# Twelve stages on one core: how each stage's semaphores are set back to zero

## The chip, the cores and the metric

The kernel runs on one core of one Trainium2 chip. The metric is the device time of one execution in microseconds (us); lower is better. Five engines work side by side, each with its own stream of instructions: TensorE (PE, with its weight loads PEld), VectorE (DVE), ScalarE (ACT), GpSimd (POOL) and SyncE (SP). SP computes nothing here: it issues most of the DMAs and handles semaphores. The engines know of each other only by semaphores, counters that one of them raises and another waits for.

## The reference, cut to what matters

All is computed in float32 on a sequence of 512 positions with 1024 features. Two layers of a first block (feed-forward, token mixing, feed-forward), then one layer of a second block (another token mixing, then a layer that picks 128 experts of 16384 for every position):

```python
def first_block(x, c, w_ada, b_ada, ...):
    c_act = jax.nn.silu(c)
    for l in range(DEPTH):                       # DEPTH = 2
        mod = (c_act @ w_ada[l] + b_ada[l])[:, None, :]
        sh0, sc0, g0, sh1, sc1, g1, sh2, sc2, g2 = jnp.split(mod, N_MOD, axis=-1)
        h = _rmsnorm(x, norm_g[l, 0]) * (1.0 + sc0) + sh0
        x = x + 0.5 * g0 * _swiglu(h, ffn_w_gate[l, 0], ffn_w_up[l, 0], ffn_w_down[l, 0])
        h = _rmsnorm(x, norm_g[l, 1]) * (1.0 + sc1) + sh1
        x = x + g1 * _token_mix(h, w_in[l], w_out[l], ...)
        h = _rmsnorm(x, norm_g[l, 2]) * (1.0 + sc2) + sh2
        x = x + 0.5 * g2 * _swiglu(h, ffn_w_gate[l, 1], ffn_w_up[l, 1], ffn_w_down[l, 1])
    return _rmsnorm(x, final_g)

def second_block(x, ...):
    for l in range(DEPTH_2):                     # DEPTH_2 = 1
        m = token_mix(x, w_in[l], ...)
        x = layer_norm(DEEPNORM_ALPHA * x + m, ln1_g[l], ln1_b[l])
        f = peer_ffn(x, peer_wq[l], peer_keys[l], peer_u[l], peer_v[l])
        x = layer_norm(DEEPNORM_ALPHA * x + f, ln2_g[l], ln2_b[l])
    return x
```

The change touches nothing of what is computed.

## The kernel before, in words

The activations stay in the core's on-chip memory (SBUF) from start to end, as `xT` (128 partitions x 8 tiles of features x 512 positions). The weights stream in from memory in tiles of 128 x 1024 numbers (512 KB). The class `Stream` moves a tile through a ring: SP loads it (`load`, the DMA at L242) into one of two raw buffers, ACT rounds it (`whi`, L252), POOL subtracts to get the rest (`wlo`, L256), and PE multiplies three times with the halves (L263 to L265), 24 matmuls to a tile. Three tiles are ready and a fourth has landed when a stage begins; `ahead` tells that to the new stage's counters, each engine raising those that are its own (SP raises `w_in`, the counters of landed tiles).

The program is a row of stages: `first_modulation`; then a hardware loop of two turns, one for each layer, over `ffn` (0), `proj_mix`, `soft_attention`, `out_proj` and `ffn` (1); then `second_mix` and `peer`. The loop's body stands in the program once, so all counters have to be zero again when the second turn comes. Each stage is one `nc.Block`: every engine jumps to its own part, runs it, and at the end all engines wait for each other (in listings, a wait for `barrier_..._release`). Inside a stage each engine's part is written out in order, so its order is that of the code.

Every stage takes its semaphores from the pool of the chip (`semaphores`, L91) and gives them back at its end, so that the next one gets the same ones. Before that, `clear` (L101) opens a block of its own with one part only, SP's, which sets them to zero one by one with `sem_clear` (L108). That block too ends with all engines waiting for each other. So between two stages there are two meetings of all engines, with SP's clears between them: 23 after `first_modulation`, 30 after `ffn`, 37 after `proj_mix`, 23 after `soft_attention`, 14 after `out_proj`, 47 after `second_mix`; none after `peer`. With the loop's two turns that is 12 clearing blocks in an execution.

PE keeps multiplying constants at the end of most stages and at the start of the next (`keep_busy`, L295; in `peer` L1973): work without a result, put there to hold up its clock.

Of the kernel before, what the change touches and what calls it, by code (L numbers as in the profile page):

```python
# [89 lines left out]

def semaphores(nc, ctx, names):  # L91

    sems = {}
    for n in names.split():
        n, _, many = n.partition("*")
        own = [ctx.enter_context(nc.semaphore(f"{n}{k}" if many else n)) for k in range(int(many or 1))]
        sems[n] = own if many else own[0]
    return sems

def clear(nc, sems):  # L101

    with nc.Block() as block:
        @block.sync
        def _(sp):
            for own in sems.values():
                for s in own if isinstance(own, list) else [own]:
                    sp.sem_clear(s)  # L108

# [23 lines left out]
def first_modulation(nc, T):  # L133

    ROWS = 8
    with ExitStack() as ctx:
        M = semaphores(nc, ctx, "lc_c lc_silu lc_const lc_x lc_par m_row*8 m_dot m_ch n_sq n_sum n_root n_rstd "
                                "w_in*2 w_hi w_lo")
# [4 lines left out]
        with nc.Block() as block:  # L143
# [53 lines left out]
            def _(dve):  # L197
# [15 lines left out]
                modulate(nc, T, link, 0)  # L213
        clear(nc, M)

S_SEMS = "w_in*2 w_hi w_lo w_mm "
# [145 lines left out]

FFN_T, PROJ_T, OUT_T = 2 * KF + 3 * KD, NZ, KD
LAYER_T = 2 * FFN_T + PROJ_T + OUT_T

def ffn(nc, T, layer, which):
# [10 lines left out]
    KL = 16  # L379
    with ExitStack() as ctx:  # L380
        M = semaphores(nc, ctx, N_SEMS + S_SEMS + Q_SEMS + "f_silu f_prod f_ahi f_act f_res f_par f_ch f_lam f_exp f_pre "
                                                           "m_row*3 m_early*2 m_dot m_raw")
        sb = lambda n, s, t=F32: ctx.enter_context(nc.sbuf_tensor(n + str(which), s, t))
# [25 lines left out]
        with nc.Block() as block:  # L409
            @block.sync  # L410
            def _(sp):
                W.ahead(sp=sp)
                if EARLY:
                    for g in range(2):
                        sp.dma_start(erow[:, g], T.d["ada"][mod_layer, 8 + g]).then_inc(M["m_early"][g], 16)
                    with sp.Fori(1, EARLY) as i:
                        for j in range(4):
                            W.load(sp, i, j)
                        for g in range(2):

                            sp.wait_ge(M["m_dot"], i * 4 + 2 * g - 1)
                            sp.dma_start(erow[:, g], T.d["ada"][mod_layer, i * 2 + 8 + g]).then_inc(M["m_early"][g], 16)
                with sp.Fori(max(EARLY, 1), KF // 2) as i:
                    for j in range(4):
                        W.load(sp, i, j)
                if which:
                    sp.dma_start(T.par[:, :], T.d["par"][1 - layer]).then_inc(M["f_par"], 16)
                for n in range(UP, UP + 3):
                    W.load(sp, n // 4, n % 4)
                rows = 0  # L430
                for o in range(KD):
                    while rows < dots // 2 and 2 * rows < sum(split[:o + 1]):
                        if rows < 3:

                            sp.wait_ge(M["w_mm"], UP + 4)
                        else:
                            sp.wait_ge(M["m_dot"], 4 * EARLY + 2 * (rows - 3) + 3)
                        sp.dma_start(wrow[:, rows % 3], T.d["ada"][mod_layer, col0 // 2 + rows]
                                     ).then_inc(M["m_row"][rows % 3], 16)
                        rows += 1  # L440
                    for n in range(UP + 3 + 3 * o, min(UP + 6 + 3 * o, FFN_T + 4)):
                        W.load(sp, n // 4, n % 4)
                W.load(sp, (FFN_T + 3) // 4, 3)
                for n in (2, 3):
                    W.landed(sp, FFN_T + n)
# [67 lines left out]
            def _(dve):  # L513
# [67 lines left out]
                Q.rstd(dve)  # L581
        clear(nc, M)

# [5 lines left out]
def proj_mix(nc, T, layer):  # L589

    with ExitStack() as ctx:
        M = semaphores(nc, ctx, N_SEMS + S_SEMS + "n_h p_rope p_wt p_tmm p_tout z_act z_dve "
                                "r_w r_rot r_t1 r_rope r_ch r_var r_root r_tri r_vn r_gelu r_sq r_sg r_y r_sig "
# [37 lines left out]
        with nc.Block() as block:  # L631
            @block.sync
            def _(sp):
                W.ahead(sp=sp)
                sp.dma_start(wtok, T.d["wtok"][layer]).then_inc(M["p_wt"], 16)
# [173 lines left out]
            def _(dve):  # L809
# [93 lines left out]
                for a in range(2):  # L903
                    dve.wait_ge(M["z_act"], ROPED + a + 1)
                    dve.wait_ge(M["r_y"], a + 1)
                    nc.vector.tensor_tensor(T.y[:, a], T.z[:, GU + a], T.y[:, a], ALU.mult)
        clear(nc, M)

def soft_attention(nc, T):  # L910
# [16 lines left out]
    with ExitStack() as ctx:  # L927
        M = semaphores(nc, ctx, "a_s a_nm a_e a_pr a_ch a_t a_te a_pv a_o "
                                "a_cs a_cm a_ce a_cp a_ct a_cte a_gate b_sq b_sum b_mean b_root b_wide b_mm b_y")
# [23 lines left out]
        SUM0 = 256  # L953
        with nc.Block() as block:
            @block.tensor
            def _(pe):
# [156 lines left out]
            def _(dve):  # L1113
# [109 lines left out]
                out(TILES - 1)  # L1223
        clear(nc, M)

def out_proj(nc, T, at):

    with ExitStack() as ctx:
        M = semaphores(nc, ctx, S_SEMS + Q_SEMS + "x_hi x_lo o_res o_pre")  # L1230
        yh = ctx.enter_context(nc.sbuf_tensor("o_yh", [P, KD, S], F32R))
# [8 lines left out]
        with nc.Block() as block:  # L1240
            @block.sync
            def _(sp):
                W.ahead(sp=sp)
                for n in range(4, OUT_T + 4):
# [42 lines left out]
            def _(dve):  # L1287
# [6 lines left out]
                Q.rstd(dve)  # L1294
        clear(nc, M)

# [6 lines left out]
def second_mix(nc, T):  # L1303
# [19 lines left out]
    with ExitStack() as ctx:  # L1323
        M = semaphores(nc, ctx, S_SEMS + "x_f x_hi x_lo p_wt v_tmm z_act z_dve "
                                "v_w v_pad v_diag v_ch v_conv v_dmm v_dc v_win v_pool v_mu v_cen v_sq v_var v_root v_rcp "
# [51 lines left out]
        with nc.Block() as block:  # L1377
            @block.sync
            def _(sp):
                W.ahead(sp=sp)  # L1380
                sp.dma_start(pw[:, :, :], T.d["pw"]).then_inc(M["v_w"], 16)
# [269 lines left out]
            def _(dve):  # L1651
# [127 lines left out]
                nc.vector.reciprocal(T.rstd[:, :], T.rstd[:, :]).then_inc(M["l_r"], 1)  # L1779
        clear(nc, M)  # L1780

# [45 lines left out]
def peer(nc, T):  # L1827
# [12 lines left out]
    with ExitStack() as ctx:  # L1840
        M = semaphores(nc, ctx, S_SEMS + f"x_t x_n x_hi x_lo e_keys e_q e_sc e_sv e_top e_ch e_x e_xo g_uv*{LOW + TOPS + EARLY} "
                                "g_dot g_gelu g_w g_diag g_mm g_ln g_al g_ch g_st g_cp g_rt g_fin g_out h_dif h_exp h_pick")
# [29 lines left out]
        with nc.Block() as block:  # L1872
            @block.sync
            def _(sp):
                W.ahead(sp=sp)
                for n in range(4, NQ2):
# [301 lines left out]
def build(nc, d):  # L2178

    T = Tensors()  # L2180
    T.d = d
    with ExitStack() as ctx:
        sb = lambda n, s: ctx.enter_context(nc.sbuf_tensor(n, s, F32))
# [49 lines left out]
def first_block(nc, T):  # L2233

    with ExitStack() as c1:
# [5 lines left out]
        T.raw = s1("raw", [P, 112])  # L2241
        T.lam = s1("lam", [P, 16])
        first_modulation(nc, T)
        with nc.Fori(0, L) as layer:
            ffn(nc, T, layer, 0)
# [152 lines left out]
```

## Time and profile before

| | |
|---|---|
| median of 3 executions | 3887.87 us (3886.22 to 3887.95) |
| the profiled execution, its own time | 3886.95 us |
| its span, from first to last instruction | 3885.2 us |
| mean granted clock of TensorE | 0.962 of full speed |
| PE busy | 3486.6 us, 90% of the span |
| DVE, POOL, ACT busy | 56%, 41%, 31% |
| DMA | 839.57 MB, mean 216 GB/s; 421 GB/s in most of `peer` |

The stages of the profiled execution, from the timeline (us from the span's start): `first_modulation` to 45, `ffn` 47 to 416, `proj_mix` 419 to 581, `soft_attention` 584 to 720, `out_proj` 722 to 774, `ffn` 775 to 1145; the second turn 1151 to 2250; `second_mix` 2253 to 2465; `peer` 2468 to 3885. In a table of windows each row gives, for one stretch, the busy time of every engine with its number of instructions in brackets, then the granted clock of PE (1.00 is full speed), the share of the DMA engines and the GB/s moved. In a timeline each row gives a start, a length, the engine, the line of the code, the operation, and in square brackets how long the engine had been idle and what ended that. "PEq L103" there stands for the clearing block: the wait ended when all had come to its end.

### The profile page before, as it was taken

What the parts mean: (1) busy time and instruction counts of PE and PEld (TensorE: products, weight loads), DVE (VectorE), ACT (ScalarE), POOL (GpSimd) and SP (SyncE); (2) the same over time, 40 slices, a digit from 0 to 9 for tenths busy, and PEclk for the clock granted to TensorE, in tenths of its full rate; (3) what the DMA queues carried; (4) which work ended last, traced back from release to release, by engine and by line L of the source; (5) the groups of instructions that cost most, each with busy time, mean ns of one, the idle gap of its engine ahead of it and who ended that gap; (6) DMA issues with size and microseconds to landing.
All of it is one profiled execution on the core that took longest, in us unless ns stands there. A gap on an engine that the chain in (4) does not pass through costs nothing. (4 is left out here: it accounts for less than half of the span.)

```text
span 3885.2 us, 41685 instructions
## 1 busy us (share of the span) xinstructions
PE 3486.6 (90%) x13886; PEld 2361.7 (61%) x13886; DVE 2174.4 (56%) x4271; ACT 1216.5 (31%) x2225; POOL 1606.3 (41%) x960
## 2 busy tenths in 40 slices
PE   6999999899999999999999999897778778777777
PEld 4888676688878887766788876663333333333332
DVE  6546257433326455466333265478677777667664
ACT  3332226443323323145333233432222222222221
POOL 3446330244545455210444632335444444444442
PEclk9999999999999999999999999998998998999998
DMA  6526320122435454200223421269999999999996
GB/s 243 194 95 259 110 98 1 45 97 97 166 126 184 146 201 179 98 17 16 88 97 112 179 82 49 93 255 408 421 422 421 421 421 422 421 421 421 420 420 275
DMA packets 141434, 839.57 MB, mean 216 GB/s; under 512 B 15824, under 2 KB 16464, under 8 KB 63952
## 3 DMA queue, kind: packets, MB, share of 16 engines
q0 software_dynamic: 73728, 536.90, 33.5%
q1 hardware_dynamic: 67536, 300.56, 21.5%
q8 instruction: 87, 1.43, 0.2%
q14 instruction: 83, 0.68, 0.1%
HBM read 835.31 MB, written 2.10 MB: 216 GB/s over the span
## 5 line engine op out<-in xcount | busy, mean ns | idle before, releaser
L256 POOL TENSOR_TENSOR wlo<-wraw,whi 128x1024 fp32r<-128x1024 f32 x357 | 906.2, 2543 | 1462.9 <-ACT whi L252 1462.6
L252 ACT ACTIVATE whi<-wraw 128x1024 fp32r<-128x1024 f32 x357 | 377.4, 1058 | 663.4 <-DMA wraw<-in_wts 371.8
L263 PE MATMUL f_ps<-f_hh,whi 128*128 128x512 f32 x1408 | 550.3, 391 | 0.9 <-DVE f_hl L352 0.9
L264 PE MATMUL f_ps<-f_hl,whi 128*128 128x512 f32 x1408 | 548.2, 389 | 0.0
L265 PE MATMUL f_ps<-f_hh,wlo 128*128 128x512 f32 x1408 | 548.1, 389 | 0.0
L1967 PE MATMUL g_psF<-g_low,g_diagb 128*128 128x512 f32 x660 | 327.6, 650 | 101.0 <-ACT g_diagb L2025 100.9
L1967 PE MATMUL g_psF<-g_own,g_diagb 128*128 128x512 f32 x576 | 279.8, 636 | 71.9 <-ACT g_diagb L2025 71.9
L521 DVE TENSOR_TENSOR f_a<-f_sg,f_ps 128x512 f32<-128x512 f32 x88 | 60.5, 688 | 503.6 <-PE f_ps L265 487.1
L1967 PE MATMUL g_psF<-g_top,g_diagb 128*128 128x512 f32 x524 | 261.8, 651 | 72.3 <-ACT g_diagb L2025 72.2
L1967 PEld LDWEIGHTS g_psF<-g_low,g_diagb 128*128 128x128 f32 x660 | 134.7, 208 | 288.9 <-issue 288.9
L2019 ACT ACTIVATE g_dotb<-g_dotb 128x4 f32<-128x4 f32 (+1 forms) x134 | 27.5, 205 | 898.4 <-DVE g_dotb L2109 898.4
L263 PEld LDWEIGHTS f_ps<-f_hh,whi 128*128 128x128 f32 x1408 | 264.7, 188 | 60.0 <-issue 3.9
L264 PEld LDWEIGHTS f_ps<-f_hl,whi 128*128 128x128 f32 x1408 | 264.7, 188 | 55.1 <-issue 0.7
L265 PEld LDWEIGHTS f_ps<-f_hh,wlo 128*128 128x128 f32 x1408 | 264.6, 188 | 55.0
L1901 POOL DMA_INDIRECT g_low<-in_uv,idx x165 | 194.5, 1179 | 220.1 <-PE g_psF L1967 185.8
L2109 DVE CUSTOM_DVE_ANT_0 g_low<-g_low,xtok 128x1024 f32<-128x1024 f32 x165 | 199.6, 1225 | 106.9 <-DMA g_low<-in_uv,idx 104.1
L1967 PEld LDWEIGHTS g_psF<-g_own,g_diagb 128*128 128x128 f32 x576 | 115.5, 205 | 228.9 <-issue 228.7
L1901 POOL DMA_INDIRECT g_own<-in_uv,idx x144 | 169.5, 1177 | 189.1 <-PE g_psF L1967 161.2
L1967 PEld LDWEIGHTS g_psF<-g_top,g_diagb 128*128 128x128 f32 x524 | 107.1, 209 | 222.2 <-issue 222.2
L2109 DVE CUSTOM_DVE_ANT_0 g_own<-g_own,xtok 128x1024 f32<-128x1024 f32 x144 | 175.9, 1237 | 94.2 <-DMA g_own<-in_uv,idx 91.0
L1901 POOL DMA_INDIRECT g_top<-in_uv,idx x131 | 148.6, 1134 | 179.6 <-PE g_psF L1967 156.8
L130 DVE CUSTOM_DVE_ANT_0 m_prod<-m_wrow,crow 128x1024 f32<-128x1024 f32 x104 | 183.7, 1767 | 50.6 <-DMA m_wrow<-in_ada 40.4
(400 smaller groups left out, 6396.9 us busy)
## 6 DMA issues: line engine op xcount, KB each, us to landing
wraw<-in_wts SPq DMA_DIRECT2D x360, 512.0 KB, 3.3
m_wrow<-in_ada SPq DMA_DIRECT2D x52, 1024.0 KB, 6.8
m_erow<-in_ada SPq DMA_DIRECT2D x28, 1024.0 KB, 5.0
p_wt<-in_wtok SPq DMA_DIRECT2D x2, 3168.0 KB, 10.5
p_wt<-in_w SPq DMA_DIRECT2D x2, 3072.0 KB, 9.7
g_low<-in_uv,idx POOLq DMA_INDIRECT x165, 24.8
g_own<-in_uv,idx POOLq DMA_INDIRECT x144, 24.3
g_top<-in_uv,idx POOLq DMA_INDIRECT x131, 24.8
```

Source lines behind the costliest of these rows:

```text
L130: nc.vector.tensor_tensor_reduce(prod, row, T.crow[:, :], 1.0, 0.0, ALU.mult, ALU.add, out).then_inc(M["m_dot"], 1)
L252: self.nc.scalar.activation(self.T.whi[:, j % 4], self.T.wraw[:, j % 2], ACT.Copy).then_inc(self.M["w_hi"], 1)
L256: self.nc.gpsimd.tensor_tensor(self.T.wlo[:, j % 4], self.T.wraw[:, j % 2], self.T.whi[:, j % 4].bitcast(F32), ALU.subtract).then_inc(self ...
L263: self.nc.tensor.matmul(out, hi, xh, start=first, stop=False)
L264: self.nc.tensor.matmul(out, hi, xl, start=False, stop=False)
L265: return self.nc.tensor.matmul(out, lo, xh, start=False, stop=last)
L521: nc.vector.tensor_tensor(a32[:, g], sg[:, g], ps[:, 2 * g + 1], ALU.mult).then_inc(M["f_prod"], 1)
L1901: nc.gpsimd.indirect_dma_start(slots[slot_of[j]], None, T.d["uv"], bass.IndirectOffsetOnAxis(ap=T.idx[:, j // TOP, j % TOP:j % TOP + 1], a ...
L1967: mm = nc.tensor.matmul(psF[:, t % 2, c], diag[:, s % 4, k], slots[slot_of[j]][:, D + c * S:D + (c + 1) * S], start=False, stop=j % (PH * ...
L2019: nc.scalar.activation(dot[:, s % 4, 0:size], dot[:, s % 4, 0:size], ACT.Gelu_apprx_tanh).then_inc(M["g_gelu"], 1)
L2109: nc.vector.tensor_tensor_reduce(u, u, xtok[:, j // (PH * TOP)], 1.0, 0.0, ALU.mult, ALU.add, dot[:, s % 4, k:k + 1]).then_inc(M["g_dot"], 1)
```

## The change

Each stage now has semaphores of its own, and the two neighbours never share any. SP zeroes those of the stage before at the beginning of its part in the next stage, ahead of its loads, and `clear` with its block is gone. `Handover` keeps the set of the stage before alive until then (`leave` gives back the set before the last). `ffn` (1), the last stage of the loop, has a set that is taken before the loop and kept, since `ffn` (0) and `second_mix` both zero it. `soft_attention`, which had no part for SP, gets one for the clears alone. One block that only clears is left, after `first_modulation`. The instructions of PE, DVE, ACT and POOL stand in the same order as before. The core of the diff (the other stages change in the same two places as `ffn`):

```diff
-def semaphores(nc, ctx, names):
+def semaphores(nc, ctx, names, stage):
...
-def clear(nc, sems):
-
-    with nc.Block() as block:
-        @block.sync
-        def _(sp):
-            for own in sems.values():
-                for s in own if isinstance(own, list) else [own]:
-                    sp.sem_clear(s)
+def zero(sp, sems):
+
+    for own in sems.values():
+        for s in own if isinstance(own, list) else [own]:
+            sp.sem_clear(s)
+
+
+class Handover:
+
+
+    def __init__(self):
+        self.before, self.now = None, None
+
+    def take(self, nc, stage, names):
+        ctx = ExitStack()
+        self.now = (ctx, semaphores(nc, ctx, names, stage))
+        return self.now[1]
+
+    def use(self, sems):
+        self.now = (None, sems)
+        return sems
+
+    def zero_before(self, sp):
+        if self.before is not None:
+            zero(sp, self.before[1])
+
+    def leave(self):
+        if self.before is not None and self.before[0] is not None:
+            self.before[0].close()
+        self.before = self.now
...
 def ffn(nc, T, layer, which):
-        M = semaphores(nc, ctx, N_SEMS + S_SEMS + Q_SEMS + "f_silu f_prod f_ahi f_act f_res f_par f_ch f_lam f_exp f_pre "
-                                                           "m_row*3 m_early*2 m_dot m_raw")
+        M = T.sems.use(T.ffn_last) if which else T.sems.take(nc, "ffn", FFN_SEMS)
...
             @block.sync
             def _(sp):
+                T.sems.zero_before(sp)
                 W.ahead(sp=sp)
...
-        clear(nc, M)
+        T.sems.leave()
...
 def soft_attention(nc, T):
         with nc.Block() as block:
+            @block.sync
+            def _(sp):
+                T.sems.zero_before(sp)
+
...
 def first_block(nc, T):
+        T.ffn_last = semaphores(nc, c1, FFN_SEMS, "ffn_last")
         first_modulation(nc, T)
+        with nc.Block() as block:
+            @block.sync
+            def _(sp):
+                T.sems.zero_before(sp)
+        T.sems.use(T.ffn_last)
+        T.sems.leave()
         with nc.Fori(0, L) as layer:
```

SP's instructions between `ffn` (0) and `proj_mix`, before (L108 is a `sem_clear`, L104 and L103 the jumps into and out of the clearing block, L635 the first DMA of `proj_mix`, L242 a load of a weight tile):

```order
142 L104 UNCONDITIONAL_BRANCH [waits barrier_Pool_Activation_PE_DVE_SP_release]
143 L108 ISA x30
144 L103 UNCONDITIONAL_BRANCH
145 L632 UNCONDITIONAL_BRANCH [waits barrier_Pool_Activation_PE_DVE_SP_release]
146 L635 ISA
147 L635 DMA p_wt<-in_wtok 128x6336
148 L242 ISA [waits w_lo]
```

The same place in the changed kernel, whose line numbers are higher by 22 to 25 there (L105 is the `sem_clear`, L656 the jump into SP's part of `proj_mix`, L660 its first DMA, L264 the load of a tile):

```order
143 L656 UNCONDITIONAL_BRANCH [waits barrier_Pool_Activation_PE_DVE_SP_release]
144 L105 ISA x30
145 L660 ISA
146 L660 DMA p_wt<-in_wtok 128x6336
147 L264 ISA [waits ffn_w_lo]
```

One of the two meetings is gone, and the 30 clears stand behind the one that is left, ahead of the first DMA. SP's instructions around `soft_attention`, before (37 clears, then the stage in which SP has nothing, then 23):

```order
191 L104 UNCONDITIONAL_BRANCH [waits barrier_Pool_Activation_PE_DVE_SP_release]
192 L108 ISA x37
193 L103 UNCONDITIONAL_BRANCH
194 L104 UNCONDITIONAL_BRANCH [waits barrier_Pool_Activation_PE_DVE_SP_release]
195 L108 ISA x23
196 L103 UNCONDITIONAL_BRANCH
197 L1241 UNCONDITIONAL_BRANCH [waits barrier_Pool_Activation_PE_DVE_SP_release]
```

And in the changed kernel (L980 is SP's new part in `soft_attention`, L1270 its part of `out_proj`):

```order
190 L980 UNCONDITIONAL_BRANCH [waits barrier_Pool_Activation_PE_DVE_SP_release]
191 L105 ISA x37
192 L979 UNCONDITIONAL_BRANCH
193 L1270 UNCONDITIONAL_BRANCH [waits barrier_Pool_Activation_PE_DVE_SP_release]
194 L105 ISA x23
195 L264 ISA [waits out_proj_w_lo]
196 L264 DMA wraw<-in_wts 128x1024
```

The 37 clears now run beside the work of `soft_attention`, and the 23 beside that of `out_proj`.

## Rows read from the trace of the kernel before

**Rows 1.** The page: its first line and PE's busy time.
```profile
span 3885.2 us, 41685 instructions
PE 3486.6 (90%) x13886; PEld 2361.7 (61%) x13886; DVE 2174.4 (56%) x4271; ACT 1216.5 (31%) x2225; POOL 1606.3 (41%) x960
```
**Rows 2.** Windows of `proj_mix`, `ffn` (1) and `peer`: PE, PEld, DVE, ACT, POOL.
```profile
418.00:581.00 163.00, 161.77 (x720) 120.03 (x720) 74.56 (x102) 41.72 (x54) 53.95 (x33) 1.00 0.30 108
...
775.00:1145.00 370.00, 368.60 (x1610) 302.85 (x1610) 126.88 (x125) 123.39 (x131) 176.73 (x74) 1.00 0.35 120
...
2468.00:3885.00 1417.00, 1116.69 (x2614) 514.26 (x2614) 979.18 (x2487) 332.42 (x822) 628.71 (x525) 0.91 0.94 387
```
**Rows 3.** Timeline, `out_proj` to `ffn` (1), 14 clears between.
```profile
770.40 3.35 DVE L331 RECIPROCAL rstd<-rstd 128x512 f32<-128x512 f32 x1 [2.60 <-ACT rstd L327]
775.20 1.42 DVE L348 SCALAR_TENSOR_TENSOR f_sg<-xT,gain,rstd 128x512 f32<-128x512 f32 x2 [1.45 <-PEq L103]
```
**Rows 4.** Timeline, `soft_attention` to `out_proj`, 23 clears; then ACT's first tile.
```profile
717.56 1.98 PE L295 MATMUL a_psS<-const 128*128 128x512 f32 x4
721.56 1.10 PE L295 MATMUL o_ps<-const 128*128 128x512 f32 x2 [2.02 <-PEq L103]
725.89 1.05 ACT L252 ACTIVATE whi<-wraw 128x1024 fp32r<-128x1024 f32 x1
```
**Rows 5.** Timeline, `ffn` (0) to `proj_mix`, 30 clears; then POOL's next two tiles.
```profile
412.97 3.35 DVE L331 RECIPROCAL rstd<-rstd 128x512 f32<-128x512 f32 x1 [2.60 <-ACT rstd L327]
418.62 1.42 DVE L348 SCALAR_TENSOR_TENSOR y<-xT,gain,rstd 128x512 f32<-128x512 f32 x2 [2.29 <-PEq L103]
418.84 0.33 SPq L635 DMA_DIRECT2D p_wt<-in_wtok  x1
435.85 4.75 POOL L256 TENSOR_TENSOR wlo<-wraw,whi 128x1024 fp32r<-128x1024 f32 x2 [3.46 <-ACT whi L252]
```
**Rows 6.** Timeline, `proj_mix` to `soft_attention`, 37 clears between.
```profile
579.09 1.89 PE L295 MATMUL r_psR<-const 128*128 128x256 f32 x8
583.59 1.28 ACT L1079 ACT_TABLE_LOAD   x1 [4.56 <-PEq L103]
```
**Rows 7.** Timeline, `second_mix` to `peer`, 47 clears between.
```profile
2461.85 3.35 DVE L1779 RECIPROCAL rstd<-rstd 128x512 f32<-128x512 f32 x1 [5.08 <-ACT rstd L1611]
2468.45 1.29 DVE L2144 TENSOR_TENSOR e_qb<-xT,rstd 128x512 f32<-128x512 f32 x2 [3.24 <-PEq L103]
```
**Rows 8.** Timeline, around the loop's way back, 30 clears between.
```profile
1141.45 3.35 DVE L331 RECIPROCAL rstd<-rstd 128x512 f32<-128x512 f32 x1 [2.60 <-ACT rstd L327]
1151.07 1.41 DVE L348 SCALAR_TENSOR_TENSOR f_sg<-xT,gain,rstd 128x512 f32<-128x512 f32 x2 [6.27 <-issue]
```
**Rows 9.** Timeline, out of the loop to `second_mix`, 30 clears between.
```profile
2246.99 3.35 DVE L331 RECIPROCAL rstd<-rstd 128x512 f32<-128x512 f32 x1 [2.60 <-ACT rstd L327]
2253.27 1.41 DVE L1679 SCALAR_TENSOR_TENSOR xT<-xT,q,rstd 128x512 f32<-128x512 f32 x2 [2.93 <-PEq L103]
```
**Rows 10.** Timeline, `proj_mix` of the second turn: its first and last instructions.
```profile
1523.28 1.41 DVE L348 SCALAR_TENSOR_TENSOR y<-xT,gain,rstd 128x512 f32<-128x512 f32 x2 [2.29 <-PEq L103]
1684.75 1.89 PE L295 MATMUL r_psR<-const 128*128 128x256 f32 x8
```
**Rows 11.** Windows at stage starts; the third number from the right is PE's clock.
```profile
418.00:425.00 7.00, 5.90 (x21) 3.98 (x22) 6.25 (x10) 3.56 (x5) 0.00 (x0) 1.00 0.75 282
...
719.00:725.00 6.00, 3.43 (x12) 1.81 (x11) 2.62 (x5) 3.29 (x7) 0.00 (x0) 1.00 0.27 89
...
775.00:780.00 5.00, 4.74 (x10) 2.60 (x11) 4.60 (x7) 2.34 (x4) 0.00 (x0) 0.66 0.30 105
...
1523.00:1527.00 4.00, 3.58 (x5) 1.69 (x6) 3.59 (x6) 2.10 (x3) 0.00 (x0) 0.57 0.65 196
```
**Rows 12.** Timeline, `peer`: POOL's first tile, and SP's DMA of the keys.
```profile
2481.58 2.39 POOL L256 TENSOR_TENSOR wlo<-wraw,whi 128x1024 fp32r<-128x1024 f32 x1 [32.19 <-ACT whi L252]
2484.38 0.42 SPq L1879 DMA_DIRECT2D e_keysb<-in_keys  x1
```

More of the change, by code:

```diff
@@ L95, in semaphores @@
         n, _, many = n.partition("*")
-        own = [ctx.enter_context(nc.semaphore(f"{n}{k}" if many else n)) for k in range(int(many or 1))]
+        own = [ctx.enter_context(nc.semaphore(f"{stage}_{n}{k}" if many else f"{stage}_{n}")) for k in range(int(many or 1))]
         sems[n] = own if many else own[0]
     return sems
-def clear(nc, sems):
-    with nc.Block() as block:
-        @block.sync
-        def _(sp):
-            for own in sems.values():
-                for s in own if isinstance(own, list) else [own]:
-                    sp.sem_clear(s)
+def zero(sp, sems):
[19 more added lines that the diff above has]
+        self.before = self.now
 def modulate(nc, T, link, n):
@@ L136, in first_modulation @@
     with ExitStack() as ctx:
-        M = semaphores(nc, ctx, "lc_c lc_silu lc_const lc_x lc_par m_row*8 m_dot m_ch n_sq n_sum n_root n_rstd "
+        M = T.sems.take(nc, "first", "lc_c lc_silu lc_const lc_x lc_par m_row*8 m_dot m_ch n_sq n_sum n_root n_rstd "
                                 "w_in*2 w_hi w_lo")
@@ L364 @@
 FFN_T, PROJ_T, OUT_T = 2 * KF + 3 * KD, NZ, KD
+FFN_SEMS = (N_SEMS + S_SEMS + Q_SEMS + "f_silu f_prod f_ahi f_act f_res f_par f_ch f_lam f_exp f_pre "
+            "m_row*3 m_early*2 m_dot m_raw")
 LAYER_T = 2 * FFN_T + PROJ_T + OUT_T
@@ L581, in _ @@
                 Q.rstd(dve)
-        clear(nc, M)
+        T.sems.leave()
 Z_ORDER = (KC, KC + 1, VC, VC + 1, NQ, NQ + 1, NQ + 2, NQ + 3, KS, KW, DQ, DQ + 1, DK, DK + 1, GU, GU + 1)
@@ L591, in proj_mix @@
     with ExitStack() as ctx:
-        M = semaphores(nc, ctx, N_SEMS + S_SEMS + "n_h p_rope p_wt p_tmm p_tout z_act z_dve "
+        M = T.sems.take(nc, "proj_mix", N_SEMS + S_SEMS + "n_h p_rope p_wt p_tmm p_tout z_act z_dve "
                                 "r_w r_rot r_t1 r_rope r_ch r_var r_root r_tri r_vn r_gelu r_sq r_sg r_y r_sig "
@@ L906, in _ @@
                     nc.vector.tensor_tensor(T.y[:, a], T.z[:, GU + a], T.y[:, a], ALU.mult)
-        clear(nc, M)
+        T.sems.leave()
 def soft_attention(nc, T):
@@ L927, in soft_attention @@
     with ExitStack() as ctx:
-        M = semaphores(nc, ctx, "a_s a_nm a_e a_pr a_ch a_t a_te a_pv a_o "
+        M = T.sems.take(nc, "soft_attention", "a_s a_nm a_e a_pr a_ch a_t a_te a_pv a_o "
                                 "a_cs a_cm a_ce a_cp a_ct a_cte a_gate b_sq b_sum b_mean b_root b_wide b_mm b_y")
@@ L1223, in _ @@
                 out(TILES - 1)
-        clear(nc, M)
+        T.sems.leave()
 def out_proj(nc, T, at):
     with ExitStack() as ctx:
-        M = semaphores(nc, ctx, S_SEMS + Q_SEMS + "x_hi x_lo o_res o_pre")
+        M = T.sems.take(nc, "out_proj", S_SEMS + Q_SEMS + "x_hi x_lo o_res o_pre")
         yh = ctx.enter_context(nc.sbuf_tensor("o_yh", [P, KD, S], F32R))
@@ L1242, in _ @@
             def _(sp):
+                T.sems.zero_before(sp)
                 W.ahead(sp=sp)
@@ L1294, in _ @@
                 Q.rstd(dve)
-        clear(nc, M)
+        T.sems.leave()
 Z_TILES = ("G0", "G1", "A0", "A1", "Q0", "K0", "PI0", "PI1", "Q1", "K1", "CH0", "CH1", "GC0", "GC1", "GB0", "GB1")
@@ L1323, in second_mix @@
     with ExitStack() as ctx:
-        M = semaphores(nc, ctx, S_SEMS + "x_f x_hi x_lo p_wt v_tmm z_act z_dve "
+        M = T.sems.take(nc, "second_mix", S_SEMS + "x_f x_hi x_lo p_wt v_tmm z_act z_dve "
                                 "v_w v_pad v_diag v_ch v_conv v_dmm v_dc v_win v_pool v_mu v_cen v_sq v_var v_root v_rcp "
@@ L1379, in _ @@
             def _(sp):
+                T.sems.zero_before(sp)
                 W.ahead(sp=sp)
@@ L1779, in _ @@
                 nc.vector.reciprocal(T.rstd[:, :], T.rstd[:, :]).then_inc(M["l_r"], 1)
-        clear(nc, M)
+        T.sems.leave()
 def choose(nc, T, B, link, dve, M, n):
@@ L1840, in peer @@
     with ExitStack() as ctx:
-        M = semaphores(nc, ctx, S_SEMS + f"x_t x_n x_hi x_lo e_keys e_q e_sc e_sv e_top e_ch e_x e_xo g_uv*{LOW + TOPS + EARLY} "
+        M = T.sems.take(nc, "peer", S_SEMS + f"x_t x_n x_hi x_lo e_keys e_q e_sc e_sv e_top e_ch e_x e_xo g_uv*{LOW + TOPS + EARLY} "
                                 "g_dot g_gelu g_w g_diag g_mm g_ln g_al g_ch g_st g_cp g_rt g_fin g_out h_dif h_exp h_pick")
@@ L1874, in _ @@
             def _(sp):
+                T.sems.zero_before(sp)
                 W.ahead(sp=sp)
@@ L2181, in build @@
     T.d = d
+    T.sems = Handover()
     with ExitStack() as ctx:
@@ L2242, in first_block @@
         T.lam = s1("lam", [P, 16])
+        T.ffn_last = semaphores(nc, c1, FFN_SEMS, "ffn_last")
         first_modulation(nc, T)
+        with nc.Block() as block:
+            @block.sync
+            def _(sp):
+                T.sems.zero_before(sp)
+        T.sems.use(T.ffn_last)
+        T.sems.leave()
         with nc.Fori(0, L) as layer:
```

## The prediction, made before the changed kernel had run

> **What bounds the kernel now.** I read the page first, then windows stage by stage, then the timeline around the stage boundaries. PE is busy for 3486.6 of 3885.2 us [rows 1]. That average hides two kinds of stages. Up to 2250 us PE is the bound nearly everywhere: 161.77 us busy of 163 in `proj_mix`, 368.60 of 370 in `ffn` (1) [rows 2]. In `peer` PE has 1116.69 of 1417 us, and the DMA engines are at 0.94 [rows 2]: the gathers are the bound there.
>
> Between two stages, however, no engine works. After the last instruction of `ffn` (0), a DVE one that ends at 412.97 + 3.35 = 416.32, nothing runs until DVE starts `proj_mix` at 418.62 [rows 5]. That hole of 2.30 us is on every path, since all engines meet in it. A shorter hole moves all that follows forward, `peer` with its gathers included, because nothing in `peer` is tied to anything but its own start.
>
> **The size of the holes.** I measured each from the end of the last engine to finish to the start of the first of the next stage, and put the number of clears beside it:
> - 14 clears: 770.40 + 3.35 = 773.75 to 775.20, so 1.45 us [rows 3]
> - 23: 719.54 to 721.56, 2.02 us [rows 4]
> - 30: 2.30 us [rows 5]
> - 37: 580.98 to 583.59, 2.61 us [rows 6]
> - 47: 2465.20 to 2468.45, 3.25 us [rows 7]
>
> From the first to the last, 33 more clears cost 1.80 us: 0.0545 us a clear. Taken off the first, 14 x 0.0545 = 0.76 leaves 0.69 us without any clear. By this line the three between would be 1.94, 2.33 and 2.71, so it holds within 0.10. The slopes between single pairs go from 0.59/14 = 0.042 (23 to 37 clears) to 0.95/17 = 0.056 (30 to 47), and these are my bounds for a clear. Two holes are longer than their 30 clears ask for: the way back of the loop, 1144.80 to 1151.07, 6.27 us [rows 8], and the way out of it, 2250.34 to 2253.27, 2.93 us [rows 9]. What they have on top, 3.97 and 0.63 us, is the jump, which stays.
>
> **The change part by part.**
>
> Removed from the path: the clears. Of 12 clearing blocks one is kept (after `first_modulation`, 23 clears), so 11 go. Their clears: 30 + 37 + 23 + 14 + 30 = 134 in a turn, 268 in two, and 47 after `second_mix`: 315. At 0.0545 us that is 17.2 us; by the bounds 13.2 to 17.6. They don't vanish: SP runs them at the head of the next stage, and what covers them is that stage's own beginning (see the next part).
>
> Removed from the path: one of two meetings of all engines at 11 places. The 0.69 us holds two meetings and SP's jumps into and out of the block. The trace has no boundary with one meeting, so the share that goes is between nothing and all of it, 0 to 7.6 us in sum. Both meetings do the same, so I take half, 0.35 us, nearest to what two equal parts make: 11 x 0.35 = 3.8 us.
>
 No row here shows a jump alone.
>
> Moved: the clears on SP, ahead of its `sem_inc` of `w_in` and of its first DMAs. The longest run is 47, 2.6 us; at `proj_mix` it is 30, 1.6 us. Against today each first DMA is issued 1.6 us later as seen from its stage's start, but 0.35 us earlier as seen from the stage before. Queued behind SP are the loads of the ring and, in `proj_mix`, 3168 KB of token weights. Who waits for that first:
> - ACT needs `w_in` raised for the fourth tile. The earliest is `out_proj`, where ACT rounds it at 725.89, 4.33 us after the stage's start [rows 4]; the 23 clears there take 1.3 us. In the other stages its work before that is longer.
> - The fifth tile in `proj_mix`, behind the token weights: POOL starts on it at 435.85 and, at half of 4.75 us, is done at 438.2 [rows 5]. PE takes 161.77/720 = 0.225 us a matmul [rows 2], so 5.4 us a tile, and needs the fifth no sooner than 4 tiles after the stage's start, 440.2. A delay of 1.6 us just fits, and in absolute time it isn't even a delay.
> - In `peer` the keys matter, for scores wait on them. SP issues that DMA at 2484.38, right after POOL's first tile is done (2481.58 + 2.39) [rows 12]. `peer` had begun at 2468.45 [rows 7] and SP had stood waiting for POOL since its first load, so 2.6 us of clears vanish in it.
> - `soft_attention` loads nothing; its 37 clears lie beside 136 us of work.
>
> So I cost the moved clears at nothing. Without that cover the price is in the first rival. In the first turn `ffn` (0) also clears the 30 of `ffn` (1), which nobody has used; its ring has the same margin as any `ffn`.
>
> Clock of PE: at the start of the second turn's `proj_mix` the granted clock is 0.57 in the window, in the first turn's 1.00 [rows 11], though the hole is the same 2.30 us. The stage takes 162.36 us in the first (418.62 to 580.98) and 163.36 in the second (1523.28 to 1686.64) [rows 5, 6, 10]. So starting at the lower of the two levels (1.2 instead of 2.4 GHz) costs 1.0 us. The 719 to 725 window has 1.00 after 2.02 us idle, 775 to 780 has 0.66 after a similar pause [rows 11]: after idle stretches of this length the clock falls in some cases. With holes of 0.35 us it should fall in fewer. PE-bound starts that are low now: `ffn` (1) twice, `proj_mix` in the second turn, and `second_mix`; four places of up to 1.0 us. In turn those that are high now could become low: `proj_mix` and `out_proj` (twice), 3 us. I take half of the four, 2.0 us, and keep -3 to +4 us as ends.
>
> **The sum.** 17.2 + 3.8 + 2.0 = 23.0 us. Against the profiled execution's own 3886.95 us (span 3885.2 and 1.75 around it): 3863.9 us. The median of the runs shown is 0.9 us higher, so 3864.5 us. All low ends together give 13.2 + 0 - 3 = 10 us, all high ends 17.6 + 7.6 + 4 = 29 us; those ends are unlikely to meet, so the likeliest case has 3858 to 3872 for itself.
>
> **The rivals.**
>
> (a) SP becomes what a stage waits for: the clears stay on the path and only the meetings go. For it: SP's DMAs do stand behind the clears, and in `proj_mix` the margin is narrow. Against it: the three margins above. Gain 3.8 us at all 11 places, 3883.5 us, which can't be told from no change. Should it hold in the two `proj_mix` alone, 2 x 1.6 = 3.3 us are lost and the time is 3868, within my range.
>
> (b) Code loading, on the other side. Today engines stand still for 2 us before a stage begins, time in which the code of the next stage can be brought in. With one short meeting each engine could arrive before its code. What a jump without its code costs is seen at the loop's way back: 3.97 us over the hole of the same 30 clears [rows 5, 8]. If all 11 places paid it, that is 43.7 us, less 21.0: 3910 us, slower. It turns the sign from 21.0/11 = 1.9 us a place. Against it: the way out of the loop, where the code goes on right behind, has only 0.63 us on top [rows 9], and the stages stand in the program one behind the other. The page "Runtime: NRT & Kernel Launch" of the Trainium skill, section Instruction fetch mechanics, says that a taken branch to code outside the two pages held stalls until that page is fetched, and that fetching ahead is sequential. The trace agrees as to the long jump [rows 8]; by the same rule a jump to the code right behind is not held up, which speaks for my forecast.
>
> (c) The clock's phase goes the other way: holes shorter, but more starts at the lower level, 3 us lost instead of 2.0 won: 3869.5 us, inside the range.
>
> (d) The stages before `peer` gain, and `peer` gives it back since it runs at the DMA engines' pace. Against it: its gathers come from indices that `peer` itself computes, so nothing could have been fetched sooner. Then the time would be 3887; I give it next to nothing.
>
> **How the numbers follow.** The forecast with (c) and the partial (a): 0.91. Full (a) or something near it, also (d): 0.06. (b): 0.03. What a measurement of this kernel can tell from no change is about 0.2%, 7.8 us, so the line is at 3880. Faster 0.91, no change 0.06, slower 0.03. The range that holds the time 8 times in 10 takes in single ends of the sum and the partial (a): 3857 to 3875 us.
>
> **What would show it.** Right: the holes at the boundaries within 0.7 us of one another's length whatever the number of clears (about 0.35 us, the way back some 4.3, its way out 1.0); stage lengths as before within 1 us; the first DMA of `proj_mix` about 1.6 us after DVE's first instruction; ACT's rounding of the fourth tile in `out_proj` still 4.3 us after the start. Wrong: holes that still grow with the clears (a), long idle times ended by "issue" at stage starts (b), or PE waiting for `wlo` early in `proj_mix`. If the holes are 0.7 us instead of 0.35, the meeting is what costs and not the number of meetings, and 3.8 us of the sum are gone.

## The result, and the profile after

| | before | changed |
|---|---|---|
| median | 3887.91 us (3886.22 to 3889.91, 4 runs) | 3864.80 us (3860.00 to 3866.86, 4 runs) |
| ratio | | 0.9943, 95% interval 0.9931 to 0.9954 |
| profiled execution, its span | 3886.95, 3885.2 us | 3866.86, 3865.1 us |

The changed kernel is 23 us faster (3864.5 was forecast); the whole interval lies beyond the 0.2% that stand for no change. Five later executions had a median of 3864.37 us.

The timeline of the changed kernel at the places of [rows 3 to 9], two or three rows to a boundary (start, length, engine, line, operation, idle time before it). The line numbers are 22 to 32 higher:

```profile
765.36 3.35 DVE L353 RECIPROCAL rstd<-rstd 128x512 f32<-128x512 f32 x1 [2.60 <-ACT rstd L349]
769.13 1.41 DVE L370 SCALAR_TENSOR_TENSOR f_sg<-xT,gain,rstd 128x512 f32<-128x512 f32 x2 [0.41 <-PEq L1269]
...
714.35 1.98 PE L317 MATMUL a_psS<-const 128*128 128x512 f32 x4
716.67 4.28 ACT L1283 ACTIVATE o_yh<-y 128x512 fp32r<-128x512 f32 x8 [5.33 <-PEq L979]
720.85 1.05 ACT L274 ACTIVATE whi<-wraw 128x1024 fp32r<-128x1024 f32 x1
...
414.07 3.35 DVE L353 RECIPROCAL rstd<-rstd 128x512 f32<-128x512 f32 x1 [2.60 <-ACT rstd L349]
417.76 1.41 DVE L370 SCALAR_TENSOR_TENSOR y<-xT,gain,rstd 128x512 f32<-128x512 f32 x2 [0.34 <-PEq L432]
419.68 0.33 SPq L660 DMA_DIRECT2D p_wt<-in_wtok  x1
434.99 2.41 POOL L278 TENSOR_TENSOR wlo<-wraw,whi 128x1024 fp32r<-128x1024 f32 x1 [3.45 <-ACT whi L274]
...
578.22 1.89 PE L317 MATMUL r_psR<-const 128*128 128x256 f32 x8
580.37 1.28 ACT L1108 ACT_TABLE_LOAD   x1 [2.21 <-DVEq L655]
...
2444.41 3.35 DVE L1810 RECIPROCAL rstd<-rstd 128x512 f32<-128x512 f32 x1 [5.09 <-ACT rstd L1642]
2448.08 1.29 DVE L2176 TENSOR_TENSOR e_qb<-xT,rstd 128x512 f32<-128x512 f32 x2 [0.32 <-PEq L1407]
...
1134.85 3.35 DVE L353 RECIPROCAL rstd<-rstd 128x512 f32<-128x512 f32 x1 [2.60 <-ACT rstd L349]
1142.37 1.19 PE L317 MATMUL f_ps<-const 128*128 128x512 f32 x1 [4.39 <-issue]
...
2230.41 3.35 DVE L353 RECIPROCAL rstd<-rstd 128x512 f32<-128x512 f32 x1 [2.60 <-ACT rstd L349]
2234.24 1.41 DVE L1710 SCALAR_TENSOR_TENSOR xT<-xT,q,rstd 128x512 f32<-128x512 f32 x2 [0.48 <-PEq L432]
```

The reader is to see two things. The holes no longer grow with the number of clears: 0.42 us where there were 1.45, 0.34 for 1.99 and 2.30, 0.26 for 2.61, 0.33 for 3.25. And the clears are on SP: its first DMA in `proj_mix` comes 1.92 us after DVE's first instruction (419.68 against 417.76), where it came 0.22 us after it [rows 5]. ACT rounds the fourth tile of `out_proj` 4.2 us after the stage's start (716.67 to 720.85), as before (4.3).

All twelve holes in order, in us, each from the last end of any engine to the next start of any. Weight loads of PE count as well, so some begin 0.03 us earlier than in the prediction; the sums are of rounded numbers and good to 0.03:

| | clears | before | changed | again | meeting kept | clears x4 | before, clears x2 | loop written out, no block |
|---|---|---|---|---|---|---|---|---|
| `first_modulation` to `ffn` (0) | 23 | 2.15 | 2.16 | 2.15 | 2.15 | 6.80 | 3.46 | 0.49 |
| to `proj_mix` | 30 | 2.30 | 0.34 | 0.34 | 0.67 | 0.34 | 4.01 | 0.34 |
| to `soft_attention` | 37 | 2.61 | 0.26 | 0.26 | 0.59 | 0.26 | 5.09 | 0.26 |
| to `out_proj` | 23 | 1.99 | 0.34 | 0.34 | 0.76 | 0.34 | 3.29 | 0.35 |
| to `ffn` (1) | 14 | 1.45 | 0.42 | 0.41 | 0.75 | 0.41 | 2.25 | 0.41 |
| way back | 30 | 6.27 | 4.14 | 3.98 | 4.30 | 3.67 | 7.89 | 0.42 |
| way out, to `second_mix` | 30 | 2.93 | 0.48 | 0.48 | 0.82 | 0.48 | 4.60 | 0.33 |
| to `peer` | 47 | 3.25 | 0.32 | 0.33 | 0.65 | 0.33 | 6.38 | 0.32 |
| sum with the second turn's four | | 31.26 | 9.81 | 9.64 | 13.46 | 13.98 | 51.62 | 4.27 |

Between the first two profiles the holes give 21.45 us and the span 20.1, so the stages themselves have become 1.3 us longer in sum (1.1 up to `peer`, 0.3 in it).

### The profile page after: what moved, and what is told of

It reads as the page before. It is cut to its first block and busy times, and to the rows that moved or that the text cites. A ratio compares the mean times of both kernels' runs of the same rounds, so it can differ in the third digit from the quotient of the medians.

```text
span 3865.1 us, 41584 instructions
## 1 busy us (share of the span) xinstructions
PE 3491.8 (90%) x13886; PEld 2362.1 (61%) x13886; DVE 2176.0 (56%) x4271; ACT 1216.8 (31%) x2225; POOL 1605.7 (42%) x960
```

## The experiments

Each was run against the kernel before on the same chip.

**The changed kernel again.** No edit.

> The changed kernel once more, with five rounds. My theory: 21 us come from the holes between stages (31.3 us in sum before, 9.8 now in the first profile), and PE's clock moves single stages by 1 us either way, so 3860 to 3868 us, median near 3865, and the same holes within 0.05 us each. If the clock takes back more in other executions, the median is nearer 3868.

Measured: 3864.37 us (3860.16 to 3869.18, 5 runs) against 3888.78 (9 runs), ratio 0.9939, interval 0.9926 to 0.9953. All holes agree within 0.02 us but the way back, 3.98 for 4.14. The spread of 9 us between executions is wider than I expected of the same program.

**What does a meeting cost?**

```diff
-    def leave(self):
+    def leave(self, nc):
+        with nc.Block() as block:
+            @block.sync
+            def _(sp):
+                pass
         if self.before is not None and self.before[0] is not None:
```

> The changed kernel with one more meeting of all engines after each of the 11 stages (a block in which nobody has work), no clears in it. My theory (a meeting costs 0.35 us): holes of 0.7 instead of 0.34 us, 11 x 0.35 = 3.9 us more, 3868 to 3869 us. Rival (nearly all of the 0.69 us in the holes without clears was the jumps into and out of SP's part, a meeting is almost free): holes of 0.4 us, 3865 to 3866. Rival (the second meeting brings the whole 0.69): holes of 1.0 us, 3872.

Measured: 3863.89 us (3861.64 to 3865.36, 4 runs), ratio 0.9936, interval 0.9921 to 0.9951. In time it can't be told from the changed kernel (3868 to 3869 were expected), in the holes it can. DVE before and after the boundary to `proj_mix` in this kernel's timeline:

```profile
413.23 3.35 DVE L357 RECIPROCAL rstd<-rstd 128x512 f32<-128x512 f32 x1 [2.60 <-ACT rstd L353]
417.25 1.41 DVE L374 SCALAR_TENSOR_TENSOR y<-xT,gain,rstd 128x512 f32<-128x512 f32 x2 [0.67 <-PEq L128]
```

0.67 us for 0.34: the second meeting costs 0.33, and over the 11 places 13.46 - 9.64 = 3.82 us, 0.35 each. The half that I took is confirmed. This kernel also isolates the clears, since the kernel before has the same two meetings at these 11 places and differs in the clears alone: its holes there are 29.11 us in sum, the ones here 11.31, so 315 clears cost 17.8 us.

That the time is no longer has another reason, the stages: `soft_attention` took 134.39 and 134.33 us here and 135.96 and 135.98 in the run above, 3.2 us less in sum, and the two `ffn` (0) 1.7 us less; `second_mix` and `out_proj` took back 1.5 and 0.4. The windows of `soft_attention`, the changed kernel's first profile first (its start, then a stretch 47 to 59 us in; the clock is the third number from the right):

```profile
580.37:588.37 8.00, 7.93 (x64) 6.05 (x64) 5.03 (x20) 4.71 (x18) 0.00 (x0) 1.00 0.00 0
627.00:639.00 12.00, 10.51 (x62) 7.41 (x60) 7.38 (x23) 6.78 (x17) 0.00 (x0) 0.72 0.00 1
```

and the one with the meetings kept:

```profile
580.18:588.18 8.00, 7.96 (x64) 6.05 (x64) 5.03 (x20) 4.74 (x18) 0.00 (x0) 1.00 0.00 0
627.00:639.00 12.00, 10.13 (x72) 7.12 (x73) 8.80 (x28) 8.47 (x19) 0.00 (x0) 0.86 0.00 0
```

Both start the stage at full clock and both fall in its middle, the one for longer. The stage has the same 1066 matmuls in both; it only began 0.2 us earlier in the first turn and 0.6 us in the second.

**Are the moved clears really covered?** Every clear of the changed kernel four times:

```diff
     for own in sems.values():
         for s in own if isinstance(own, list) else [own]:
-            sp.sem_clear(s)
+            for _ in range(4):
+                sp.sem_clear(s)
```

> The changed kernel with every clear made four times. SP then clears for 6.5 us at the start of proj_mix, 8.1 in soft_attention, 5.0 in out_proj, 3.1 and 6.5 in the two ffn, 10.2 in peer. My theory (the clears are covered): only the block kept after first_modulation shows them, its hole grows by 69 x 0.0545 = 3.8 us; PE may wait up to 3 us for the fifth weight tile in each proj_mix. 3869 to 3875 us. Rival (the clears are still on the path, partly or wholly): 945 + 69 more clears give up to 55 us, 3880 to 3920 us.

Measured: 3866.98 us (3865.86 to 3869.70, 4 runs), ratio 0.9944, interval 0.9929 to 0.9959. The first hole grew by 4.65 us for 69 clears (0.067 each), as it must where the clearing block was kept. The other eleven did not grow, though 1035 clears more were made behind them. SP's queue, POOL and PE in `proj_mix`, whose first DVE instruction is at 422.63:

```profile
430.11 0.34 SPq L661 DMA_DIRECT2D p_wt<-in_wtok  x1
430.65 0.33 SPq L265 DMA_DIRECT2D wraw<-in_wts  x1
431.04 0.42 SPq L663 DMA_DIRECT2D rope<-in_rope  x1
434.00 2.40 POOL L279 TENSOR_TENSOR wlo<-wraw,whi 128x1024 fp32r<-128x1024 f32 x1 [19.66 <-ACT whi L275]
442.94 2.39 POOL L279 TENSOR_TENSOR wlo<-wraw,whi 128x1024 fp32r<-128x1024 f32 x1 [6.54 <-ACT whi L275]
447.36 3.17 PE L771 MATMUL p_psT<-p_wt,y 128*128 128x512 f32 x7
```

The first DMA comes 7.48 us after the stage's start and the stage still takes 162.34 us (as in the changed kernel). PE did not wait here, and the last row shows why the margin is wider than I had worked out: after four tiles, 24.7 us into the stage, PE does not go to the fifth tile but to the token weights `p_wt`. SP had issued their load 17.2 us earlier, and it takes some 10 us to land. The fifth tile, ready at 445.33, is wanted only after them.

**Is it the clears that made the holes?** The kernel before, each clear twice:

```diff
                 for s in own if isinstance(own, list) else [own]:
                     sp.sem_clear(s)
+                    sp.sem_clear(s)
```

> The kernel before with every clear made twice. My theory (0.0545 us a clear, all on the path): holes grow by 0.76, 1.25, 1.64, 2.02 and 2.56 us for 14, 23, 30, 37 and 47 clears; 338 more clears give 18.4 us, 3906 us, with a clock that starts low in more stages (up to 3 us on top). Rival (the holes are long for another reason that goes with a stage, the clears are nearly free): holes as before, 3888 us.

Measured: 3914.46 us (3912.71 to 3915.34, 4 runs), ratio 1.0068, interval 1.0053 to 1.0084: 25.7 us more. The 14 clears to `ffn` (1) and the 47 to `peer`, in DVE's rows of this kernel:

```profile
781.64 3.35 DVE L332 RECIPROCAL rstd<-rstd 128x512 f32<-128x512 f32 x1 [2.60 <-ACT rstd L328]
787.24 1.41 DVE L349 SCALAR_TENSOR_TENSOR f_sg<-xT,gain,rstd 128x512 f32<-128x512 f32 x2 [2.25 <-PEq L103]
...
2497.38 1.29 DVE L2145 TENSOR_TENSOR e_qb<-xT,rstd 128x512 f32<-128x512 f32 x2 [6.38 <-PEq L103]
```

Idle for 2.25 against 1.45 us, and 6.38 against 3.24 [rows 3, 7]. Per added clear that is 0.80/14 = 0.057 us, 1.71/30 = 0.057, and 2.48/37 and 3.13/47 = 0.067. All holes together grew by 20.4 us; the stages up to `peer` took another 8.6 us more, and `peer` gave 3.2 back.

The trace also records every clear on SP, which neither the prediction nor the expectations used. In the kernel before their starts are 0.057 us apart. But here and there two neighbours are 0.36 to 0.46 us apart instead (in two profiles one pair behind the jump back 1.0 and 1.2 us). In the kernel before two of the 12 rows of clears have such a gap, both at the loop's end: the way back (0.42 us at 1145.36) and the way out (0.42 us at 2250.88). The 30 clears after `ffn` (0) beside the 30 of the way out (number, shortest, median and longest in ns, first and last start):

```profile
L108 SPq EVENT_SEMAPHORE_RANGE_CLEAR  x30: 25/28/30, 416.6 to 418.3; - x30
L108 SPq EVENT_SEMAPHORE_RANGE_CLEAR  x30: 25/30/38, 2250.6 to 2252.8; - x30
```

With the clears doubled, the rows of 74 and of 94 have one such gap each too (0.38 to 0.41 us), the shorter ones away from the loop's end none. So 0.067 is 0.057 and a gap, and not a higher price for each clear. The 4.65 us of the fourfold run before are 69 x 0.057 = 3.9, a gap of 0.4 more than usual, and 0.3 that stay open. In the run with ten times the clears, gaps within one row of clears are 128 clears (7.7 us) apart; what makes them was not tested.

With holes of 2.3 to 7.9 us all 12 stages began below full clock, at a mean of 0.57 to 0.81 in their first 8 us. In the kernel before it was 8 of the 12.

**Without the last clearing block.** The semaphores of `first_modulation` stay its own and aren't cleared:

```diff
-        M = T.sems.take(nc, "first", "lc_c lc_silu ...")
+        M = T.sems.use(semaphores(nc, T.keep, "lc_c lc_silu ...", "first"))
...
         first_modulation(nc, T)
-        with nc.Block() as block:
-            @block.sync
-            def _(sp):
-                T.sems.zero_before(sp)
         T.sems.use(T.ffn_last)
```

> The changed kernel without its last clearing block: the 23 semaphores of first_modulation stay its own to the end of the program and are never cleared, since that stage runs once. My theory (holes of one meeting are 0.34 us, and PE's clock starts a stage low only behind the long ones): the first hole goes from 2.15 to 0.3 us, ffn (0) of the first turn starts with a granted clock nearer 1.00 and takes 369.6 instead of 370.7 us; 1.8 + 1.1 = 2.9 us less than the changed kernel, 3861 to 3862. Rival (ffn (0) is longer because SP's 30 clears delay its loads, not by the clock): the stage stays at 370.7 us, 3862.6 us. In either case PE had been at the lower level before that hole, so the clock may stay low there by itself.

Measured: 3861.54 us (3859.29 to 3863.14, 5 runs), ratio 0.9932, interval 0.9919 to 0.9946. Against the changed kernel's ratio of 0.9939 the intervals overlap, so the time alone does not show a gain; the hole does, 0.59 for 2.15. `ffn` (0) of the first turn took 369.99 us for 370.71, but that of the second 372.02 for 370.80. The latter is not the clock, which was higher there (0.79 against 0.62 in the first 8 us). DVE and PE of this kernel at the start of that turn:

```profile
1141.60 1.42 DVE L370 SCALAR_TENSOR_TENSOR f_sg<-xT,gain,rstd 128x512 f32<-128x512 f32 x2 [6.98 <-issue]
1144.04 0.47 PE L285 MATMUL f_ps<-f_hh,whi 128*128 128x512 f32 x1 [1.74 <-DVE f_hl L374]
```

After the jump back DVE starts 2.98 us later than PE's first constants (1138.62), and PE then waits 1.74 us for it; in the changed kernel DVE was there 0.05 to 0.24 us after PE, and no such wait appears. So the way back costs more than its hole says, and another amount each time.

My theory of the clock failed in the first turn. Behind a hole of 0.59 us the stage still began at 0.73, while the kernel before began it at 1.00 behind 2.16 us. In both PE had been at 0.50 in the last 4.6 us of `first_modulation`, so neither that nor the length of the hole decided.

**The loop written out.**

```diff
-        with nc.Fori(0, L) as layer:
+        names = nc
+        for layer in range(L):
+            nc = Renamed(names, layer) if layer else names
             ffn(nc, T, layer, 0)
```

(`Renamed` only gives the second turn's buffers and semaphores other names.)

> The changed kernel with the two turns of the loop written out in the program one behind the other (no jump back, twice the code). My theory (the way back's hole of 4.1 us is 0.34 for the meeting and 3.8 for the jump to code that is far back): that hole falls to 0.34 us, and ffn (0) of the second turn starts at full clock, 370.8 to 370.0; the way out falls by 0.1. 4.6 us less than the changed kernel, 3860 us. Rival for the hole (it is the work of all engines at the loop's end, not the jump): it stays near 4. Against me: more code has to be brought in, which may show as idle time ended by 'issue' elsewhere.

Measured: 3854.26 us (3852.08 to 3854.67, 5 runs), ratio 0.9913, interval 0.9900 to 0.9927: some 10 us less than the changed kernel, twice what I expected. At the place of the way back:

```profile
1132.71 3.35 DVE L353 RECIPROCAL rstd<-rstd 128x512 f32<-128x512 f32 x1 [2.60 <-ACT rstd L349]
1136.48 1.41 DVE L370 SCALAR_TENSOR_TENSOR f_sg_t<-xT,gain,rstd 128x512 f32<-128x512 f32 x2 [0.42 <-PEq L432]
```

0.42 us for 3.98: the jump was 3.6 us of that hole, and twice the code shows in no other hole. The second turn's `ffn` (0) took 369.02 us for 370.80, the first's 369.46 for 370.71, one `soft_attention` 134.99 for 135.96: 4.0 us less, each at a higher mean clock (in that `soft_attention` 0.99 against 0.97). This run also settles why `ffn` (0) had become longer. SP makes the same 30 clears at its start here, so it is not they. The windows of its first 16 us and of the second turn's first 8, changed kernel:

```profile
46.80:62.80 16.00, 15.98 (x55) 11.62 (x56) 11.41 (x16) 9.01 (x11) 1.98 (x1) 0.82 0.44 166
1142.40:1150.40 8.00, 8.00 (x20) 5.04 (x21) 7.73 (x11) 4.09 (x6) 0.00 (x0) 0.64 0.68 258
```

and loop written out:

```profile
46.80:62.80 16.00, 15.06 (x60) 10.70 (x61) 11.43 (x17) 10.13 (x13) 2.00 (x1) 1.00 0.43 166
1136.50:1144.50 8.00, 7.53 (x28) 4.88 (x28) 7.73 (x11) 4.11 (x6) 0.00 (x0) 1.00 0.66 254
```

**Both.**

> Both of the last two edits on the changed kernel: no block behind first_modulation, and the loop written out. If they add up: 2.9 + 4.6 = 7.5 us less, 3857 us against 3864.5, all twelve holes between 0.26 and 0.5 us, 4 us in sum. If PE's clock takes some back in the middle of soft_attention and second_mix: 3858 to 3861.

Measured: 3851.08 us (3850.83 to 3853.46, 4 runs), ratio 0.9909, interval 0.9894 to 0.9924. This is the fastest version: 36 us under the kernel before, holes of 4.27 us in sum. Expected were 3857; the 6 us more come from the stages, as above: both `ffn` (0) at 369.7 and 369.1, both `soft_attention` at 134.35.

**Where does the cover end?** The kernel without the last clearing block, with the loop of clears of the second experiment at `range(10)`:

> The kernel of e5_no_first_block with every clear made ten times, to find where the cover ends: SP clears for 16 to 20 us at the start of proj_mix, ffn and soft_attention, 13 in out_proj, 8 in ffn (1), 26 to 31 in peer. My theory (what counts is when the first instruction is due that needs SP): ACT's fourth tile is due 4.3 us after the start of out_proj and 12 to 13 us after the start of the other stages, PE needs it some 16 us in. So PE waits a few us in each proj_mix and each ffn (0), little in out_proj, none in ffn (1) and soft_attention, and peer's keys come 10 us late: 20 to 50 us more than e5, of 2835 clears that would be 155 us on the path. Rival (a cover that is independent of the number): no loss.

Measured: 3907.19 us (2 runs), ratio 1.0052, interval 1.0033 to 1.0070, 45.7 us more than with single clears. The waits of PE in `proj_mix` and the stage around it, then in `peer`, in this kernel (who waited for whom, us in total, times, longest):

```profile
PE p_psT L771 <- DMA p_wt<-in_wtok: 2.4, 1, 2.4
PE p_psZ L286 <- POOL wlo L279: 2.2, 1, 2.2
...
PE e_psS L1964 <- DMA e_keysb<-in_keys: 22.3, 1, 22.3
ACT whi L275 <- SPq L254: 16.3, 1, 16.3
```

Now ACT waits for SP to raise `w_in`, the keys come so late that PE waits 22.3 us for them, `proj_mix` takes 169.2 us, `ffn` (0) 376.9, `second_mix` 221.9 (213.5 with single clears) and `peer` 1430.1 (1414.3). `out_proj` (52.0 us, 230 clears) and `ffn` (1) (369.05 us, 140 clears) still show nothing. So the first rival describes a real mechanism: it decides somewhere between 4 and 10 times the present number of clears.

## Why the prediction was right, point by point

**The holes.** Forecast 21.0 us (17.2 clears, 3.8 meetings), measured 21.45 and 21.62 in two profiles. The two terms are each shown by the run that keeps the meeting: 3.8 us for 11 meetings against the changed kernel, 17.8 us for 315 clears against the kernel before. The price of a clear was read from the line through five holes as 0.0545 us; the clears themselves stand 0.057 us apart in the trace. The bounds of 0.042 to 0.056 were too narrow: between neighbours among the five holes the slope runs from 0.28/7 = 0.040 to 0.64/10 = 0.064, since the holes differ in more than their clears (in the changed kernel, with no clears in them, they are 0.26 to 0.42 us long). The 0.067 of the doubled and the fourfold clears includes the single gaps shown above.

**What the jumps have on top.** I let 3.97 and 0.63 us stay [rows 5, 8, 9]. On the way back 4.14 - 0.34 = 3.80 stayed, on the way out only 0.48 - 0.34 = 0.14. So I had put down to the jump what was not all the jump's: in each of the two, 0.36 us was the gap among SP's 30 clears, and went off the path with them. The kernel with the meetings kept agrees: its way out is 0.82 us, 0.15 above the 0.67 of `proj_mix`. The rest of the 0.5 us stays open.

**The cover.** Right, with more room than I gave it. Late by 1.7 us as seen from its stage (0.22 to 1.92), SP's first DMA was waited for by no one, and not at 7.5 us either. The step that was misread is what PE wants after four tiles in `proj_mix`: the token weights, and the fifth tile only behind them. In the run with ten times the clears their load is issued 18.2 us into the stage, and PE waits for it for 2.4 us.

**PE's clock.** This term was mis-sized: +2.0 us forecast, but up to `peer` the stages lost 1.1 us in the first profile and gained 0.3 in the second. Its first half held: all ten stages behind the short holes began at 1.00 in their first 8 us, in each of the eight profiles with holes of 0.26 to 0.82 us, where the kernel before had three of the ten. The windows of the changed kernel at the stage starts of [rows 11]:

```profile
417.00:424.00 7.00, 5.95 (x22) 3.84 (x22) 6.53 (x11) 3.43 (x5) 0.00 (x0) 1.00 0.50 170
716.00:722.00 6.00, 5.25 (x20) 3.49 (x20) 4.66 (x8) 5.31 (x10) 0.02 (x1) 1.00 0.28 91
769.00:774.00 5.00, 4.39 (x15) 2.63 (x16) 4.67 (x7) 2.42 (x4) 0.00 (x0) 1.00 0.31 107
1513.00:1517.00 4.00, 3.19 (x10) 1.73 (x10) 3.54 (x6) 2.06 (x3) 0.00 (x0) 1.00 0.36 82
```

All at 1.00, where two were at 0.66 and 0.57; none that was high became low. The step that failed is "four places of up to 1.0 us". `proj_mix` of the second turn gave 1.0 (163.36 to 162.37), the two `ffn` (1) 0.5 each, `out_proj` 0.2 each, but `second_mix` nothing (211.93 to 213.52, then 211.91). And I had not counted what lies outside the short holes: the low stretches at the start of `ffn` (0), after the two long holes that stayed, became longer (in the first turn there had been none; 1.1 and 0.8 us), and `second_mix` lost 1.6 in one profile of two. The 1.1 and the 1.6 are more than the 1 us that I had allowed a stage. The two `soft_attention` had begun low too, at a mean of 0.79, and beginning at full clock took no less (135.9 to 136.0 us before and after), for the low stretch in their middle became longer. The runs show that such stretches differ between kernels and executions with the same instructions, not what sets them.

**The rivals.** (a) did not occur at this number of clears (its price of 3883.5 us should have been 3884), (d) neither: `peer` took 1417.0 us after 1416.8. (b), the slower side, is refuted for stages that stand one behind the other: holes of 0.26 to 0.48 us leave no room for a wait for code. Its price of nearly 4 us a jump is right for the one far jump, as the written-out loop shows (3.6 us, and more where an engine comes late). With the rule of the Trainium skill that I cited, "Runtime: NRT & Kernel Launch", Instruction fetch mechanics, the traces agree on both sides: the jump far back is held up, those to the code right behind are not. That the wait is for code is the page's explanation; the runs show only that it goes with the jump.

That the median came out within 0.3 us is partly luck. The two profiled executions are 20.1 and 24.5 us under that of the kernel before: 21.45 from the holes less 1.1 and 0.3 for stages and `peer`, and 21.6 + 0.3 + 2.6. The forecast of 23.0 lies between, with 0.5 us too little for the holes and 2 us too much for the clock. Why `peer`, unchanged, took 1414.2 us in one and 1417.0 in the other stays open.

## What to carry to other kernels

Measure the holes between stages from the last end of any engine to the next start of any, and plot them against what stands between: here five of them gave the price of a clear and of the rest before anything was run, and the clears' own starts on SP would have given it more directly. Bookkeeping of one idle engine (clearing semaphores) need not stand between two meetings of all; it can go to the head of the next stage if that engine's first useful instruction there has slack, and making it several times over measures how much. A loop's jump back cost more than any clearing block, so a loop of two turns is better written out where the program has room.

## What the runs showed of the hardware

- `sem_clear`s on SP stood 0.055 to 0.057 us apart, with single gaps of 0.36 to 0.46 us, 128 clears apart in the longest rows; a second meeting of all five engines at a block's end cost 0.33 to 0.41 us between stages that stand one behind the other.
- The jump back over the loop's body held the engines for 3.6 us more than going on to the code behind, and in one run DVE for some 3 us longer than PE.
- Behind holes of 0.26 to 0.82 us all ten stages that the change brought closer to their neighbours began at full clock in each of eight profiles; behind 1.45 to 3.24 us three of ten did. Behind `first_modulation`, where PE had been at 0.50, a hole of 0.59 us was followed by a mean of 0.73, one of 2.16 us once by 1.00.
- PE's clock fell in the middle of `soft_attention` for a stretch of two lengths (mean 0.72 or 0.86 over 12 us), worth 1.6 us of the stage, with the same instructions in it. Executions of one program differed by up to 9 us.
